# A transformer layer on one Trainium2 core: who casts three weight chunks, and how the second decay factor is formed

## The reference

```
h   = rmsnorm(x)
q, k, v, xr, yr, gate_logits = split(h @ w_in + b_in)
attn = grouped-query attention (8 query heads, 2 key heads, q/k norm, axial rotary)
xc   = width-4 depthwise convolution of xr
for direction in (forward, backward):          # RG-LRU
    r, i  = sigmoid(block_diag(xc, wa) + ba), sigmoid(block_diag(xc, wi) + bi)
    log_a = 8 * r * log_sigmoid(lambda)
    a     = exp(log_a)
    u     = sqrt(-expm1(2 * log_a)) * (i * xc)
    h_t   = a_t * h_(t-1) + u_t                 # a scan over the 256 tokens
rec  = (h_forward + h_backward) * gelu(yr)
x   += (sigmoid(g_A) * (attn @ w_attn_o) + sigmoid(g_R) * (rec @ w_lru_o)) @ w_out
x   += top-4 of 32 experts, each a clamped SwiGLU of width 1024
out  = rmsnorm(x)
```

## Time and profile before

| | us |
|---|---|
| median of 3 runs | 1190.94 (1190.27 to 1191.61) |
| profiled execution, its own time | 1188.62 |
| span of its instructions | 1186.8 |
| PE busy | 1082.9 (91%) |
| VectorE busy | 373.4 (31%) |
| ScalarE busy | 249.5 (21%) |
| mean granted clock of PE | 0.991 |

### The profile page before, as it was taken

The page is one execution under the profiler, slowest core; times in us unless marked ns, Lnnn a source line. Parts: engine busy times, 40 slices in busy tenths (PEclk is TensorE's granted clock), DMA queues, the critical chain, the costliest instruction groups (busy, mean ns, idle before and its releaser), DMA issues.

```text
span 1186.8 us, 13216 instructions
## 1 busy us (share of the span) xinstructions
PE 1082.9 (91%) x5391; PEld 520.3 (44%) x5392; DVE 373.4 (31%) x657; ACT 249.5 (21%) x390; POOL 0.2 (0%) x4
## 2 busy tenths in 40 slices
PE   5998989989999999999998989999999999999996
PEld 5997878843433333333333333333333333333332
DVE  6967587442222222212121212121212121212123
ACT  5397962131111111111111111111111111111112
POOL 0000000000000000000000000000000000000000
PEclk9998999989999999999999999999999999999999
DMA  8543224889999999999999999999999999999993
GB/s 348 192 153 118 96 85 199 339 329 400 430 427 427 427 428 428 430 427 430 427 430 427 429 428 429 427 429 428 429 429 428 429 428 429 428 429 428 429 428 144
DMA packets 31610, 439.89 MB, mean 371 GB/s; under 512 B 3648, under 2 KB 3776, under 8 KB 4832
## 3 DMA queue, kind: packets, MB, share of 16 engines
q1 hardware_dynamic: 31104, 438.53, 88.0%
q10 hardware_dynamic: 480, 0.99, 0.2%
HBM read 438.46 MB, written 1.05 MB: 370 GB/s over the span
## 4 chain that ended last, share of the span: by engine, by line
DMA 48%; PE 42%; DVE 4%; ACT 4%; issue 1%; SPq 0%; DVEq 0%; ACTq 0%
DMA slot<-in_w_down_dram 24%; DMA slot<-in_w_gu_dram 24%; PE ps L1243 14%; PE ps L1254 10%; PE ps L979 9%; PE ps L1220 3%; PE ps L1208 2%; PE ps L1287 1%; DVE slot_r L584 1%; PE ps L1020 1%; ACT slot_r L344 1%; PE ps L1034 1%; DMA slot<-in_pre_dram 1%; DVE lru L713 1%; ACT lru L394 1%
## 5 line engine op out<-in xcount | busy, mean ns | idle before, releaser
L1243 PE MATMUL ps<-slot,lru 128*64 128x512 f32 x896 | 203.2, 595 | 14.2 <-DMA slot<-in_w_gu_dram 13.2
L1243 PE MATMUL ps<-slot,qT 128*64 128x512 f32 x896 | 203.8, 596 | 13.3 <-DMA slot<-in_w_gu_dram 13.3
L1254 PE MATMUL ps<-slot,kT 128*64 128x512 f32 x512 | 116.8, 597 | 17.4 <-DMA slot<-in_w_down_dram 16.0
L1243 PEld LDWEIGHTS ps<-slot,lru 128*64 128x64 f32 x896 | 71.0, 137 | 134.5 <-issue 103.5
L1243 PEld LDWEIGHTS ps<-slot,qT 128*64 128x64 f32 x896 | 64.4, 136 | 127.2 <-issue 103.3
L1254 PE MATMUL ps<-slot,lru 128*64 128x512 f32 x384 | 87.5, 597 | 15.4 <-DMA slot<-in_w_down_dram 15.4
L519 ACT ACTIVATE lru<-ps 128x512 f32<-128x512 f32 x32 | 19.1, 598 | 378.2 <-PE ps L1243 378.2
L932 DVE TENSOR_TENSOR lru<-ps,cst 128x1024 f32<-128x1024 f32 x32 | 39.2, 1225 | 161.8 <-PE ps L1287 161.8
L901 DVE TENSOR_SCALAR lru<-sq,pbuf 128x64 f32<-128x64 f32 x66 | 13.8, 252 | 215.9 <-PE ps L1208 215.9
L1254 PEld LDWEIGHTS ps<-slot,kT 128*64 128x64 f32 x512 | 36.7, 136 | 94.4 <-issue 94.3
L979 PE MATMUL ps<-wide_r,slot_r 128*128 128x256 f32 x512 | 70.8, 291 | 4.9 <-issue 4.9
(11 more groups left out here) (194 smaller groups left out, 928.2 us busy)
## 6 DMA issues: line engine op xcount, KB each, us to landing
slot<-in_w_gu_dram SPq DMA_DIRECT2D x112, 2048.0 KB, 34.9
slot<-in_w_down_dram SPq DMA_DIRECT2D x56, 2048.0 KB, 35.3
wide<-in_w_gu_dram SPq DMA_DIRECT2D x16, 2048.0 KB, 33.7
slot<-in_pre_dram SPq DMA_DIRECT2D x14, 2048.0 KB, 7.9
wide<-in_w_down_dram SPq DMA_DIRECT2D x8, 2048.0 KB, 35.3
slot<-in_w_lru_dram SPq DMA_DIRECT2D x2, 1024.0 KB, 13.4
x_sb<-in_x_dram SPq DMA_DIRECT2D x2, 512.0 KB, 4.8
slot<-in_pre_dram SPq DMA_DIRECT2D x1, 1024.0 KB, 5.3
```

Of the source, the lines that this page charges most:

```text
L1243: ins = nc.tensor.matmul(ps[64 * side:64 * side + 64, 4 + b, :], xgT[i % 2][:, k, :], w[:, r, o:o + BANK], start=(k == 0), stop=(k == KD - 1))
L1254: ins = nc.tensor.matmul(ps[64 * side:64 * side + 64, 6, :], actT[(i - 1) % 2][:, k, :], w[:, r, side * BANK:(side + 1) * BANK], start=(k ...
```

## The change

- VectorE, not ScalarE, makes the high parts of chunks 5 and 9, each as one cast of 128x4096 directly ahead of the low part. The cast waits for the chunk's DMA, and the low part waits for the cast by VectorE's own step semaphore.
- ScalarE's cast of chunk 6 moves from behind part 2 of the decay of half 0 to directly behind the root of the q/k variance, ahead of groups 8 to 13 and of all decay parts.
- Part 1 of the decay in both halves is one `Square` of `lruA` over 128x2048 where it was eight exponentials of 128x256; it waits for the eight instructions of part 0.
- The counts that low parts wait for are adapted (`casts_before`), and the tensor engine waits for the low part of a chunk alone.

```diff
+        CAST_V = (5, 9)
+
+        def casts_before(c):
+            return 2 * sum(b not in CAST_V for b in range(c))
+
@@ lru_decay
-                if part < 2:
-                    dst, lam = ((lruA, lam_h), (lruE, lam_f))[part]
+                if part == 0:
                     for o, k in blocks:
-                        nc.scalar.activation(dst[:, o:o + TOK], lruR[:, o:o + TOK], ACT.Exp, scale=lam[:, k:k + 1],
-                                             bias=lam[:, k:k + 1]).then_inc(lru_x, 1)
+                        nc.scalar.activation(lruA[:, o:o + TOK], lruR[:, o:o + TOK], ACT.Exp, scale=lam_h[:, k:k + 1],
+                                             bias=lam_h[:, k:k + 1]).then_inc(lru_x, 1)
+                elif part == 1:
+                    act.wait_ge(lru_x, 9 * u + 8)
+                    nc.scalar.activation(lruE, lruA, ACT.Square).then_inc(lru_x, 1)
                 else:
-                    act.wait_ge(lru_x, 16 * (u + 1))
+                    act.wait_ge(lru_x, 9 * (u + 1))
@@ ScalarE's order
             lru_gates(0, range(4))
-            split_high(5)
             act.wait_ge(qk_inv, 1)
             nc.scalar.activation(qk_rstd, qk_rstd, ACT.Sqrt).then_inc(qk_rs, 1)
+            split_high(6)
             for i in range(8, 14):
                 group(i)
                 if i % 2 == 1:
                     lru_decay(0, i // 2 - 4)
-            split_high(6)
             copy_qk()
@@ ScalarE, attention loop
-                if i in (23, 24):
-                    split_high(9, [i - 23])
@@ VectorE
+            def split_high(c):
+                dve.wait_ge(slot_full[2 * (c % PAIRS)], 16 * (c // PAIRS + 1))
+                link(high_part(high(c), whole(c)))
+
             def split_low(c):
 
-                dve.wait_ge(split_hi, 2 * c + 2)
+                if c not in CAST_V:
+                    dve.wait_ge(split_hi, casts_before(c) + 2)
                 low_part(low(c), whole(c), high(c)).then_inc(split_lo, 1)
@@ VectorE's order
             nc.vector.reciprocal(qk_rstd, qk_rstd).then_inc(qk_inv, 1)
+            split_high(5)
             split_low(5)
@@ VectorE, attention loop
                 if s == 6:
+                    split_high(9)
                     split_low(9)
@@ tensor engine
             def chunk_in(c):
-                pe.wait_ge(split_hi, 2 * c + 2)
                 pe.wait_ge(split_lo, c + 1)
```

## The result

| | before | after |
|---|---|---|
| median, 6 runs each, side by side | 1191.12 us (1190.27 to 1193.18) | 1180.86 us (1178.24 to 1182.06) |
| ratio | | 0.9912 [0.9898, 0.9925] |
| profiled execution, span | 1186.8 | 1178.3 |

By the ratio the change saves 10.5 us (8.9 to 12.2); 8.9 was forecast. The median lies 0.1 us under the forecast's own range (1181.0 to 1183.2) and inside the 8-in-10 range. A later set of runs of the same kernel gave 0.9935 [0.991, 0.9959], 7.7 us.

The account below looks back on a forecast made before the run. Compute in the stages ahead of the DMA-full expert stream was taken to set when it begins, so savings there reach the end: 5.8 + 3.1 = 8.9 us, 1190.94 - 8.9 = 1182.0; own range 1181.0 to 1183.2, 8-in-10 range 1180.3 to 1186.0.

Parts of the forecast that it names:

- D: Expert weight stream: bound elsewhere than at its beginning, so the front gains and the end doesn't; 1190.9 us, chance 0.05.
- E: Expert weight stream, 330 to 1150 us: lower rate once it begins at another moment; slower, 1193.5 us, chance 0.04.
- The sign that I had set for D and E: From the products with the recurrent result to the end: any distance other than the old 1009.9 us.
- First half, 5.8 forecast: Recurrence, 60 to 107 us: root starts at 90.54 instead of 96.33, gate products resume at 101.85 instead of 107.65; 5.8 us.
- the new wait: Tensor engine behind group 18, near 98.7 us: stands about 3.1 us for VectorE's sum, already inside the 5.8 us gain.
- the terms written for the tensor engine: Groups 16, 17, four gate products and group 18 at full clock: 88.2 + 2x2.88 + 1.6 + 3.0, ending at 98.7.
- Rival C: VectorE casts at its subtraction's pace, 4.43 us; first half gains 5.1, second 1.0; gain 6.1, 1184.8 us, chance 0.07.
- The square: Second decay factor in both halves: one activation instead of eight saves ScalarE 2.1 us a half, hidden, worth nothing.
- Its table set: ScalarE's square might need two more table loads a half; 0.4 us in all, or an estimated 2 by the skill.
- Second half, 3.1 forecast: 107.65 to 176.93 us: chunk 9's cast on VectorE brings products with the recurrent result 3.1 us earlier, 1.0 idle left.
- rival B: Tensor engine's 3.1 us wait ends at 1.2 GHz, costing 2.6 us; gain 6.3, 1184.6 us, chance 0.21.
- I take it as kept: Clock at the 3.1 us wait: assumed to stay up, as behind 2.62 us, not fall as behind 4.64 us.

Follow-up runs that it names:

- the first half alone: Changed kernel with chunk 9's cast back on ScalarE and the eight exponentials back in place of the square; 1186.2 us, ratio 0.9962 to the old kernel.
- no square: Changed kernel with the eight exponentials of both halves put back in place of the square; 1180.8 us, ratio 0.9912 to the old kernel.
- after again: The changed kernel, unaltered, run and profiled a second time; 1181.8 us, ratio 0.9935 to the old kernel.
- cast 5 alone: Old kernel with only chunk 5's cast moved to VectorE; 1190.3 us, ratio 0.9995 to the old kernel.
- the move alone: Old kernel with only ScalarE's cast of chunk 6 moved ahead of groups 8 to 13 and the decays; 1192.1 us, ratio 1.0013 to the old kernel.

## Why the prediction was right

*Where the end is set.* From the branches to the end the old kernel needs 1009.87 us, after 1009.15. The front's gain arrives whole, and the stream runs at 428 GB/s in both; rivals D and E are out. Of the 0.7 us, 0.4 lie in the routing, up to the first expert's transposes (254.45 in before, 246.27 in after), where the clock was at 0.50 for 10 us in before and for 7 in after; 0.3 come later and were not traced. The sign that I had set for D and E, any other distance than 1009.9, was too strict: over the thirteen profiles it was 1009.2 to 1014.8.

*First half, 5.8 forecast, 5.94 measured.* The cast took 2.23 and 2.28 us against 2.28. The root stands at distance 34.8 (forecast 34.9), behind ScalarE's table load, as said; the new wait is 3.15 us against 3.1 (the terms written for the tensor engine add up to 98.6, not 98.7, and 98.6 is what the trace has, counted from the first gate product). The two experiments that leave one edit out show how they share the gain, which the sum did not split: cast 5 gives nothing alone, the move gives 4.0 us of root alone, and only both give 5.9. Rival C is out with the cast.

*The square.* Called hidden in both halves; the kernel without it has the same distances and ratio. Its table set: no load beside it at 77.97.

*Second half, 3.1 forecast, 3.22 measured*, with 1.11 us of idle left (1.0). The low part of chunk 10 starts right behind ScalarE's second piece, as worked out. Chunk 9's cast alone gives the same 3.2, so the two halves add: 5.94 + 3.22 = 9.2 in the traces against 8.9.

*The profiled execution*, 1180.86 against 1179.7: 1.4 us of it was lost ahead of the first gate product. Before's profiled execution was a fortunate one: 1188.62, with 4.09 us for the first products, where its median is 1191.12. I carried the difference of the two, 2.3 us, over unchanged; in after the profiled execution stands at the median, so that term was not there. That the median came within 1.1 us all the same is in part luck.

*What was mis-sized: rival B.* I made it one branch: either the clock is kept or it is lost at this wait. The runs show that it differs from execution to execution and from wait to wait, in the old kernel as well. The wait of 3.15 us kept the clock in three profiles (after, the first half alone, no square) and lost it in one (after again). The wait of 2.62 us kept it in two (before, cast 5 alone) and lost it in two (the first half alone, the move alone). "I take it as kept" held for the profiled execution, and that was luck. The price, put at 2.6 us, was 1.1 to 1.65 where the clock came back after three to three and a half microseconds of products, and 4.2 where it took nine. The Trainium skill (TensorE: Matmul & The Clock Gate, section "Part 1: The HAM clock gate") says that the activity check runs free of the kernel; these pairs of traces agree with it, though they don't show the cause. A fixed threshold read off two rows of one trace, as I did with 2.62 and 4.64, doesn't hold. Four profiles are too few to say how often each wait loses the clock.

## What to carry to other kernels

A cast that one engine makes and another waits for can be cheaper on the waiting engine, even when it adds busy time there: the wait for it goes, and the first engine's queue moves up. Follow such a move through every queue that the earlier consumer then meets, since the next wait may stand on an engine that nobody looked at (chunk 7's low part). And count each tensor engine wait of two microseconds and more at more than its length: filling it with independent products saves the wait and the risk of the clock behind it.

## What was not expected of the hardware

- The granted clock fell behind idle of 2.33, 2.62, 3.15, 3.78, 4.41, 4.57, 4.64 and 5.93 us, and stayed up behind 2.62 and 3.15 in other executions. Behind the 1.9 to 2.3 us ahead of the sixth branch it fell in five of the thirteen profiles, and it stayed up behind both the shortest and the longest of these waits. Within one kernel, at one instruction, this made 4.2 us.
- Where the runs of one kernel spread widely, their time goes with the mean granted clock: 1188.2 us at 0.990 and 1195.5 at 0.985 in the move of cast 6 alone, 1179.0 at 0.995 and 1188.3 at 0.988 in after again. These spreads of 7 and 9 us are nearly as large as the gain under study.
- The first 32 products of every execution took either about 4.1 or 5.8 to 6.3 us, with the same start (15.2 to 15.3) and with a granted clock of 1.00 on record for that stretch in all of them, so only the durations show it. That alone moves all later times by 1.1 to 1.7 us, so two profiles are better compared from a common instruction behind it than from the start.
